# Packed rotary columns, norm sums on VectorE, attention on queries and keys in place, in a two-block transformer kernel

## The chip, the cores and the metric

The kernel runs on one core of a Trainium2 chip. The time is that of the whole program on the device, in microseconds (us). A profiled execution also gives a span, from its first to its last instruction.

## What is computed

Two transformer blocks work on one sequence of 512 tokens of width 1024, all in f32. The first block puts 16 meta tokens in front (528 columns in all). It has an RMS norm, an input projection, an S5 state-space mixer, differential attention with 4 heads, output products, and a gated feed-forward with its own norm. The second block has two layers; each has a norm, an input projection of 28 column blocks, four branches (a conformer convolution, an HGRN2 branch, an SSD branch, latent attention with rotary positions), an output product and a norm of its result. What the change touches:

```python
def rmsnorm(x, g):
    r = lax.rsqrt(jnp.mean(xf * xf, axis=-1, keepdims=True) + EPS)
    return (xf * r).astype(x.dtype) * g
...
    # first block, attention: q and k after their norm, per head two halves of 64
    s = jnp.einsum('bqhjd,bkhjd->bhjqk', q_blk, k)
    p = jax.nn.softmax(s, axis=-1)
    w = p[:, :, 0] - lam * p[:, :, 1]
    o = jnp.einsum('bhqk,bkhe->bqhe', w, v)
...
def apply_rotary(x, positions):      # x: 32 columns; x1, x2 its halves
    out = jnp.concatenate([x1 * cos - x2 * sin, x2 * cos + x1 * sin], axis=-1)
...
def mla_branch(cq, ckv, k_rope, gate, positions, qa_g, qb_w, kva_g, kvb_w):
    q = (rms_norm(cq, qa_g) @ qb_w).reshape(bsz, s, D_HEADS, D_NOPE + D_ROPE)
    q = jnp.concatenate([q[..., :D_NOPE], apply_rotary(q[..., D_NOPE:], positions)], axis=-1)
    k_r = apply_rotary(k_rope, positions)
...
    x = x + rms_norm(y, post_norm_g[l])    # y: the output product of the layer
```

## The kernel before

Activations lie transposed: 128 channels on the partitions, tokens along the free dimension, eight tiles for 1024 channels. The residual is X, the squares and then the normed input are in HN, projections in PJ (PJ2 is the same memory in the second block, 28 tiles of 512 columns), scratch in SC, V and R. Weights stream through `ring`, four slots of 512 KB, which SyncE fills as TensorE frees them. Each engine runs its own hand-written program; the order of its lines is the order of the work, and semaphores tie the engines together. A wait therefore holds everything behind it on its engine. PSUM has eight banks: `put`/`take` wait until one is free, `full`/`got` wait until it is filled.

**A norm's sum** (`norm_sum`, L370) is a product with a matrix of ones, which adds the squares over the partitions: ScalarE squares a tile (`sq_ready`), TensorE adds it into PSUM. In the first block a tile's 528 columns are two halves of 264, and all eight tiles of half 0 come before those of half 1. Then ScalarE takes logarithm and exponential (`root`, L1105 and L1107), and VectorE scales eight tiles (`norm`, L1695), each of which lets TensorE go on. The first call stands at the program's start; VectorE computes angles up to L1742 meanwhile. The second stands behind the first block's output product (L622), whose results VectorE adds to X (L1913) and ScalarE squares (L1314); VectorE then prepares the first feed-forward weights (`sums(0)`, L1923 to L1926).

**Attention of the first block.** ScalarE copies a head's queries and keys out of PJ into QS and KS (`queries`, L1228 and L1229, semaphore `qst`). Per head and per tile of queries (t = 0 has 16, t = 1 to 4 have 128): `score` on TensorE (L505 to L514), VectorE adds the position bias and takes the maximum (L1850, L1854), ScalarE exponentiates (L1247), VectorE combines the two halves (L1868), `turn` transposes the weights (L524), ScalarE copies them (L1254, L1255), `weigh` multiplies by the values (L533). Between these stand `gate_half` products (L490) of the gate projection. Tiles 0 and 1 of the next head are scored inside the loop of this one, so the loop of head 3 scores a fifth head that nobody uses.

**Second block, start of a layer.** `part(j)` (L719) is projection j, 16 instructions, into bank 0 or 1. Projections 0 to 3 are the latent query, the latent key and a mixed tile (time steps in rows 0 to 3, rotary key in rows 64 to 95). `d_sums` sums their squares (L733, L736); ScalarE makes the root; VectorE scales them (L2019, L2020) and posts `d_mul`. The rotary needs the key with its halves swapped: a product with the matrix `rot` (L958), which ScalarE copies to R (L1433, `d_kr`). `d_query(h)` makes a head's query (L742, 96 rows) and, in a second pair of products, its swapped rotary part (L747, 32 rows), each in its bank; ScalarE copies both (L1381, L1383). GpSimd multiplies by cosine and sine and adds (L1636 to L1643): first the key, then each head's query. Behind this come projections 6 to 9, keys and values. VectorE meanwhile starts on the convolution's 31 taps (L2253, L2033, L2035) as soon as ScalarE has evacuated projection 7, and gives attention its first scores (L2042) after 14 of them.

**Second block, end of a layer.** The output product has eight tiles (L1065). ScalarE squares each from PSUM into PJ2 (L1574, `y_sq`) and copies it to HN (L1575). Behind each tile but the first, TensorE adds the squares of the tile before with a `ones` product (L1071); the last one is L1073. ScalarE then takes the root (L1577, L1579), and VectorE and GpSimd update X.

Of the kernel before, what the change touches and what calls it, by code (L numbers as in the profile page):

```python
# [49 lines left out]
CONSTS = [("ident", P), ("ones", P), ("pair64", P), ("mult", 28), ("lvl", 256), ("rot", P), ("dist", T), ("mlamask", SEQ), ("causal", P),  # L50
# [44 lines left out]
def build(nc, a, out):  # L95

    with ExitStack() as ctx:
# [24 lines left out]
        for name in ("par_in", "cst_in", "sc_far", "g_full", "ones_in", "eps_ready", "v_zero", "v_ready", "s5_dt", "ys_gelu",  # L122
# [3 lines left out]
                     "o_root", "o_norm", "glu_th", "ys_ready", "mix_ready", "h_ready", "ffa", "ffc", "ffg", "hid_done", "small_in",  # L126
                     "b_tok", "a_sq", "gate_th", "c_th", "c_x", "c_acb", "c_cme", "d_root", "d_qe", "d_trig_arg", "d_trig", "d_q",
                     "d_sc", "d_ex", "d_wt", "yo", "y_sq", "pos_in", "qst", "a_act", "a_dve", "a_mul", "b_act", "b_dve", "b_mul",
                     "b_zero", "c_act", "c_dve", "c_in", "c_mul", "c_tok", "d_kr", "d_misc", "d_mul", "d_tok", "d_tr", "g_used",
                     "par2_in", "w2_free", "x1_ready", "x2_e", "x2_o", "y_done", "sa_ready", "tb_ready", "snap", "ff_p", "ff_u", "g_free0", "g_free1"):  # L130
# [62 lines left out]
        QS = cut(T)  # L193
        KS = cut(T)
# [96 lines left out]
        def bank(b):  # L291

            return PS[b // 2][:, b % 2, :]
# [49 lines left out]
        def _(pe):  # L343
# [19 lines left out]
            def norm_sum(t0=0, halves=2, width=H):  # L363

                put(0, False)
                for h in range(halves):
                    for k in range(KD):
                        if h == 0:
                            pe.wait_ge(*n("sq_ready"))
                        ins = mm(PS[0][:, h, 0:width], c("ones"), HN[:, k, t0 + h * width:t0 + (h + 1) * width],  # L370
                                 start=(k == 0), stop=(k == KD - 1))
                ins.then_inc(SEMS["act_full0"], 1)
                n("hn_ready", KD)
# [123 lines left out]
            def score(t):  # L497
# [42 lines left out]
            pe.wait_ge(*n("qst"))  # L540
            score(0)
            score(1)
# [4 lines left out]
            for h in range(HEADS):  # L547
                g = 3 + 3 * h
                score(2)
                gate_half(g, 0)  # L550
                turn(0)
                score(3)
# [3 lines left out]
                score(4)  # L556
# [7 lines left out]
                pe.wait_ge(*n("qst"))  # L564
                score(0)
# [3 lines left out]
                score(1)  # L569
# [58 lines left out]
            norm_sum()  # L628
# [73 lines left out]
            for l in range(LAYERS):  # L702
# [35 lines left out]
                def d_query(h):  # L738
                    x, y = (6, 7) if h % 2 == 0 else (2, 3)
# [1757 lines left out]
```

## Time and profile before

| | us |
|---|---|
| median of 3 runs | 1708.13 (1707.27 to 1710.15) |
| profiled execution, its own time | 1707.5 |
| its span | 1705.7 |
| TensorE (PE) busy | 1629.5, 96% |
| VectorE (DVE) busy | 745.9, 44% |
| ScalarE (ACT) busy | 421.9, 25% |
| GpSimd (POOL) busy | 116.7, 7% |

The 1.8 us between the profiled execution's time and its span lie outside the first and last instruction. A matmul on f32 shows as two MATMUL rows, one for each of two instructions, and a row's duration runs from start to modelled end; consecutive ones overlap, so their busy time is not the sum of durations. The rows "PEld" are weight loads, which overlap the matmuls.

### The profile page before, as it was taken

The numbers are of one execution on the slowest core, as the hardware profiler recorded it, in microseconds if no ns is written. First come the engines' busy times: TensorE is split into PE (matmuls) and PEld (weight loads), VectorE is DVE, ScalarE is ACT, GpSimd is POOL, SyncE is SP. The second block draws the span as 40 slices with busy tenths as digits, with TensorE's granted clock in tenths as the row PEclk, the third lists the DMA queues.
The fourth block names the chain that finished last, engine by engine and source line by source line (L and its number), as shares of the span: only waits on it lengthen the run. The fifth ranks groups of instructions, "written<-read, shape, count | busy, mean of one in ns | idle before, by whom it ended". The sixth has DMA issues, their size and how long they took to land.

```text
span 1705.7 us, 16217 instructions
## 1 busy us (share of the span) xinstructions
PE 1629.5 (96%) x6364; PEld 1031.9 (60%) x6364; DVE 745.9 (44%) x1267; ACT 421.9 (25%) x823; POOL 116.7 (7%) x82
## 2 busy tenths in 40 slices
PE   7999999999989999999999998999998998999996
PEld 6884677778878888884443434555543434555542
DVE  8537433322137676762002047765303147765302
ACT  3652544430011010101001131242412131242321
POOL 4014000000000000000000050001001050001001
PEclk9999999999999999999999999999999999999998
DMA  5211111322212222222222212112121211111121
GB/s 203 65 38 48 49 49 50 101 90 74 73 39 81 93 83 90 85 89 86 75 74 61 63 37 62 38 50 63 49 63 38 74 37 56 44 50 38 37 74 49
DMA packets 31660, 111.60 MB, mean 65 GB/s; under 512 B 3520, under 2 KB 3776, under 8 KB 31072
## 3 DMA queue, kind: packets, MB, share of 16 engines
q1 hardware_dynamic: 31248, 108.32, 20.4%
q0 software_dynamic: 336, 2.23, 0.4%
q8 instruction: 51, 0.84, 0.2%
q14 instruction: 25, 0.20, 0.0%
HBM read 108.45 MB, written 2.10 MB: 65 GB/s over the span
## 4 chain that ended last, share of the span: by engine, by line
PE 90%; DVE 6%; ACT 2%; issue 1%; ACTq 1%; DMA 0%; POOL 0%; DVEq 0%; SPq 0%
PE PS L719 21%; PE PS L645 16%; PE PS L675 9%; PE PS L1065 6%; PE PS L490 6%; PE PS L390 5%; PE PS L609 3%; PE PS L622 3%; PE PS L466 2%; DVE SC L2035 2%; PE PS L811 2%; PE PS L370 1%; PE PS L768 1%; PE PS L747 1%; PE PS L784 1%; PE PS L742 1%
## 5 line engine op out<-in xcount | busy, mean ns | idle before, releaser
L719 PE MATMUL PS<-HN,ring 128*128 128x512 f32 x896 | 407.8, 605 | 4.9 <-DVE HN L1695 4.9
L719 PEld LDWEIGHTS PS<-HN,ring 128*128 128x128 f32 x896 | 168.9, 193 | 204.6 <-issue 199.7
L675 PE MATMUL PS<-PJ,ring 128*128 128x512 f32 x352 | 151.3, 592 | 1.9 <-DVEq L1679 1.9
L645 PE MATMUL PS<-SC 128*128 128x257 f32 x528 | 123.6, 383 | 2.0 <-issue 2.0
L675 PEld LDWEIGHTS PS<-PJ,ring 128*128 128x128 f32 x352 | 66.8, 190 | 86.0 <-issue 83.7
L1065 PE MATMUL PS<-PJ,ring 128*128 128x512 f32 x256 | 112.1, 592 | 0.0
L645 PEld LDWEIGHTS PS<-SC 128*128 128x128 f32 x528 | 101.3, 192 | 17.3 <-issue 2.4
L490 PE MATMUL PS<-HN,ring 128*128 128x264 f32 x448 | 107.0, 393 | 2.2 <-ACT PJ L1209 2.2
L390 PE MATMUL PS<-HN,ring 128*128 128x264 f32 x448 | 103.3, 391 | 2.5 <-DVE HN L1695 2.5
L390 PEld LDWEIGHTS PS<-HN,ring 128*128 128x128 f32 x448 | 85.6, 192 | 18.6 <-issue 2.9
L490 PEld LDWEIGHTS PS<-HN,ring 128*128 128x128 f32 x448 | 84.1, 192 | 19.7 <-issue 3.7
L2035 DVE SCALAR_TENSOR_TENSOR SC<-SC 128x512 f32<-128x512 f32 x120 | 84.8, 749 | 2.6
L1065 PEld LDWEIGHTS PS<-PJ,ring 128*128 128x128 f32 x256 | 48.6, 190 | 61.2 <-issue 61.2
L645 PE MATMUL PS<-HN,ring 128*128 128x257 f32 x352 | 81.6, 382 | 2.4 <-DVE HN L1695 2.4
L1326 ACT ACTIVATE SC<-PS 128x257 f32<-128x257 f32 x44 | 17.0, 386 | 240.2 <-PE PS L645 240.2
L645 PEld LDWEIGHTS PS<-HN,ring 128*128 128x128 f32 x352 | 66.1, 190 | 14.4 <-issue 2.7
L1993 DVE TENSOR_TENSOR X<-X,PS 128x1024 f32<-128x1024 f32 x4 | 4.9, 1221 | 139.4 <-PE PS L675 139.4
L622 PE MATMUL PS<-PJ,ring 128*128 128x264 f32 x256 | 57.2, 386 | 1.7 <-DVEq L1679 1.7
L609 PE MATMUL PS<-PJ,ring 128*128 128x264 f32 x256 | 57.2, 386 | 1.5 <-DVE PJ L1892 1.5
L2350 DVE SCALAR_TENSOR_TENSOR PJ<-HN,V,R 128x512 f32<-128x512 f32 x8 | 5.9, 743 | 119.4 <-ACT R L1579 119.4
L622 PEld LDWEIGHTS PS<-PJ,ring 128*128 128x128 f32 x256 | 48.6, 190 | 10.4 <-DVEq L1679 2.1
L609 PEld LDWEIGHTS PS<-PJ,ring 128*128 128x128 f32 x256 | 48.6, 190 | 10.2 <-DVE PJ L1892 1.9
(420 smaller groups left out, 2091.6 us busy)
## 6 DMA issues: line engine op xcount, KB each, us to landing
ring<-wst SPq DMA_DIRECT2D x188, 512.0 KB, 3.6
X<-xT SPq DMA_DIRECT2D x16, 264.0 KB, 5.4
V<-small POOLq DMA_DIRECT2D x2, 1024.0 KB, 5.2
outT<-X SPq DMA_DIRECT2D x8, 256.0 KB, 2.1
consts<-cst SPq DMA_DIRECT2D x1, 1291.5 KB, 13.5
V<-s5w SPq DMA_DIRECT2D x1, 1280.0 KB, 10.3
POS<-pos SPq DMA_DIRECT2D x1, 256.0 KB, 13.7
params<-par SPq DMA_DIRECT2D x1, 209.5 KB, 2.6
```

The source lines that it names most:

```text
L370: ins = mm(PS[0][:, h, 0:width], c("ones"), HN[:, k, t0 + h * width:t0 + (h + 1) * width], start=(k == 0), stop=(k == KD - 1))
L390: ins = mm(PS[p][:, h, 0:H], ring[:, k % 4, b * P:b * P + P], HN[:, b, h * H:h * H + H], start=(b == 0), stop=(b == KD - 1))
L466: ins = mm(PS[t // 2][0:rows, t % 2, :], HN[:, b, q0:q0 + rows], ring[:, b // 2, (b % 2) * 512:(b % 2) * 512 + 512], start=(b == 0), stop= ...
L490: ins = mm(PS[h][:, 1, 0:H], ring[:, k % 4, b * P:b * P + P], HN[:, b, h * H:h * H + H], start=(b == 0), stop=(b == KD - 1))
L609: ins = mm(PS[p][:, h, 0:H], ring[:, s, (4 * x + b) * P:(4 * x + b) * P + P], src, start=(b == 0), stop=(b == 3))
L622: ins = mm(PS[k][:, h, 0:H], ring[:, s, b * P:b * P + P], PJ[:, 12 + b, h * H:h * H + H], start=(b == 0), stop=(b == KD - 1))
L645: ins = mm(PS[bnk // 2][:, bnk % 2, 0:257], left[:, b * P:b * P + P], right[:, b, :], start=(b == 0), stop=(b == 3))
L675: ins = mm(PS[m // 2][:, m % 2, :], ring[:, s, m * P:m * P + P], hid[:, k, :], start=start, stop=stop)
L719: ins = mm(bank(b), ring[:, r, i * P:i * P + P], HN[:, i, 0:SEQ], start=(i == 0), stop=(i == KD - 1))
L811: ins = mm(o, BK[rows, cc, t * P:t * P + P], q, start=True, stop=True)
L1065: ins = mm(bank(j % 2), ring[:, j % WSLOTS, b * P:b * P + P], PJ2[:, src, :], start=(x == 0), stop=(x == KD - 1))
L2035: ins = stt(CA[:, cc, :], x, w1, CA[:, cc, :], ALU.mult, ALU.add)
```

## The change

It has four parts.

1. **Norm sums.** The first `norm_sum` runs tile by tile with both halves of a tile together. For the feed-forward's norm and for the norm of the output product, VectorE adds the squares of tiles 0 to 6 into tile 6 (six additions each), and TensorE multiplies only tiles 6 and 7 by ones. New semaphores `sq_sum` and `y_sum` say when tile 6 holds the sum. The `ones` products between output products go.
2. **Attention of the first block** reads queries and keys from PJ. `queries`, QS, KS and `qst` go, and head 3 no longer scores a fifth head.
3. **Rotary key.** The mixed weight tile has the swapped key columns in columns 96 to 127, so projection 3 gives both. `rot` and its product go; ScalarE copies the rows in the evacuation of projection 3, and `d_kr` goes with its wait on GpSimd.
4. **Rotary queries.** The swapped parts of the four heads are packed into 128 columns and made by one pair of products (`d_swapped`, bank 5) ahead of the queries; ScalarE copies them in four pieces of 32 rows (`swapped`). Each `d_query(h)` keeps one pair, and the heads use banks 6, 7, 2, 3.

```diff
-            def norm_sum(t0=0, halves=2, width=H):
+            def norm_sum(added=0):
                 put(0, False)
...
+                for k in range(added, KD):
+                    if k == added and added:
+                        pe.wait_ge(*n("sq_sum"))
+                        n("sq_ready", KD - 1)
+                    else:
+                        pe.wait_ge(*n("sq_ready"))
+                    for h in range(2):
+                        ins = mm(PS[0][:, h, 0:H], c("ones"), HN[:, k, h * H:(h + 1) * H], start=(k == added), stop=(k == KD - 1))
...
-                q = [QS[64 * j:64 * j + 64, q0:q0 + rows] for j in range(2)]
-                kk = [KS[64 * j:64 * j + 64, :] for j in range(2)]
+                q = [PJ[64 * j:64 * j + 64, 4 + head, q0:q0 + rows] for j in range(2)]
+                kk = [PJ[64 * j:64 * j + 64, 8 + head, :] for j in range(2)]
...
-                pe.wait_ge(*n("qst"))
-                score(0)
+                if h + 1 < HEADS:
+                    score(h + 1, 0)
...
-            norm_sum()
+            norm_sum(KD - 2)
...
                 def d_query(h):
-                    x, y = (6, 7) if h % 2 == 0 else (2, 3)
+                    x = (6, 7, 2, 3)[h]
...
+                def d_swapped():
+                    take(5)
                     for b in range(2):
+                        ins = mm(bank(5), SW[:, SWR + b * P:SWR + b * P + P], CQ[:, b, :], start=(b == 0), stop=(b == 1))
+                    ins.then_inc(SEMS["ba5"], 1)
...
-                take(4)
-                mm(bank(4), c("rot"), PJ2[:, 16, :], start=True, stop=True).then_inc(SEMS["ba4"], 1)
                 pe.wait_ge(*n("small_in", 16))
                 pe.wait_ge(*n("d_mul"))
+                d_swapped()
...
-                    if i:
-                        pe.wait_ge(*n("y_sq"))
-                        mm(bank(2), c("ones"), PJ2[:, i - 1, :], start=(i == 1), stop=False)
-                pe.wait_ge(*n("y_sq"))
+                pe.wait_ge(*n("y_sum"))
+                mm(bank(2), c("ones"), PJ2[:, KD - 2, :], start=True, stop=False)
+                pe.wait_ge(*n("y_sq", KD))
                 mm(bank(2), c("ones"), PJ2[:, KD - 1, :], start=False, stop=True).then_inc(SEMS["ba2"], 1)
...
-            def queries(h):
-                af(QS[:, :], PJ[:, h + 4, :], ACT.Copy)
-                af(KS[:, :], PJ[:, h + 8, :], ACT.Copy).then_inc(SEMS["qst"], 1)
...
+                def swapped():
+                    full(5)
+                    for h in range(HEADS):
+                        ins = af(QR[rr, h, :], bank(5)[32 * h:32 * h + 32], ACT.Copy, scale=-(QKR ** -0.5))
+                    released(ins, 5)
...
-                evac(3, 16)
+                full(1)
+                af(PJ2[:, 16, :], bank(1), ACT.Copy)
+                released(af(KRR[rr, :], bank(1)[96:128], ACT.Copy), 1)
...
-                pool.wait_ge(*n("d_kr"))
...
+                    done = i * 4 + k
+                    if done == 0:
+                        n("sq_ready", KD)
+                    if done:
+                        dve.wait_ge(*n("sq_ready"))
+                    if done > 1:
+                        link(tt(HN[:, done - 1, :], HN[:, done - 1, :], HN[:, done - 2, :], ALU.add))
+            post("sq_sum")
...
+                dve.wait_ge(*n("y_sq"))
+                for k in range(1, KD - 1):
+                    dve.wait_ge(*n("y_sq"))
+                    link(tt(PJ2[:, k, :], PJ2[:, k, :], PJ2[:, k - 1, :], ALU.add))
+                post("y_sum")
+                n("y_sq")
                 dve.wait_ge(*n("rms_root"))
...
+        misc[:, 96:128] = misc[:, 64:96][:, swap]
```

The instruction streams show two places. TensorE, layer 0 of the second block, between projection 5 and projection 7 (L742 queries, L747 their swapped parts before, L749 the packed ones now, L958 `rot`):

```order
 L719 MATMUL PS<-HN,ring 128x512 x16
-L958 MATMUL PS<-PJ,consts 128x512
-L742 MATMUL PS<-PJ,V 96x512 x2
-L747 MATMUL PS<-PJ,V 32x512 x2
-L742 MATMUL PS<-PJ,V 96x512 x2
-L747 MATMUL PS<-PJ,V 32x512 x2
+L749 MATMUL PS<-PJ,V 128x512 x2
+L742 MATMUL PS<-PJ,V 96x512 x4
 L719 MATMUL PS<-HN,ring 128x512 x8
```

Nine products between the projections became six; behind the second projection eight became four. TensorE in head 3 of the first block's attention (L505, L511 scores, L533 values, L524 transposes, L490 gates):

```order
 L490 MATMUL PS<-HN,ring 128x264 x8
-L505 MATMUL PS<-SC 16x16
-L511 MATMUL PS<-SC 16x16
 L533 MATMUL PS<-V,SC 128x128 x4
 L524 MATMUL PS<-consts,SC 128x128 x5
 L490 MATMUL PS<-HN,ring 128x264 x8
-L505 MATMUL PS<-SC 128x144
-L511 MATMUL PS<-SC 128x144
 L533 MATMUL PS<-V,SC 128x128 x5
 L490 MATMUL PS<-HN,ring 128x264 x16
```

The scores that nobody uses are gone, and with them VectorE's and ScalarE's work on them, which stood ahead of the combination that the transposes of tile 4 (L524 x5) wait for.

## Rows read from the trace of the kernel before

**Rows 1.** The page, parts 1 and 4: the engines, and the chain that ended last.
```profile
PE 1629.5 (96%) x6364; PEld 1031.9 (60%) x6364; DVE 745.9 (44%) x1267; ACT 421.9 (25%) x823; POOL 116.7 (7%) x82
...
PE 90%; DVE 6%; ACT 2%; issue 1%; ACTq 1%; DMA 0%; POOL 0%; DVEq 0%; SPq 0%
```

**Rows 2.** TensorE's waits: line <- what ended them: us in total, times, longest.
```profile
PE PS L768 <- DVE SC L2042: 4.6, 2, 2.3
```

**Rows 3.** The chain of waits, output products of layer 0: start us, us, what.
```profile
1254.23 6.87 PE PS L1065 x16
1261.95 6.87 PE PS L1065 x16
```

**Rows 4.** The norm of the feed-forward: the chain, then the timeline.
```profile
487.23 7.13 PE PS L370 x32
...
488.06 0.64 ACT L1314 ACTIVATE HN<-X 128x528 f32<-128x528 f32 x1 [6.48 <-DVEq L1675]
488.18 0.69 DVE L1923 TENSOR_TENSOR SC<-ring 128x512 f32<-128x512 f32 x1 [0.20 <-issue]
```

**Rows 5.** Timeline of layer 0's output products, ScalarE: start us, us, engine, line.
```profile
1292.03 0.60 ACT L1574 ACTIVATE PJ<-PS 128x512 f32<-128x512 f32 x1 [6.64 <-PE PS L1065]
```

**Rows 6.** The chain of waits, layer 0: the `rot` product, heads 0 and 1.
```profile
979.97 0.86 PE PS L958 x2
980.83 1.72 PE PS L742 x4
982.55 1.83 PE PS L747 x4
...
988.10 7.07 PE PS L719 x16
```

**Rows 7.** Timelines of layer 0 by engine: ScalarE, VectorE (DVE), GpSimd (POOL).
```profile
981.99 0.59 ACT L1433 ACTIVATE R<-PS 32x512 f32<-32x512 f32 x1
...
969.50 0.74 DVE L2020 SCALAR_TENSOR_TENSOR PJ<-PJ,V,SC 128x512 f32<-128x512 f32 x1
...
1010.21 1.23 DVE L2253 SCALAR_TENSOR_TENSOR SC<-PJ 128x1024 f32<-128x1024 f32 x1 [23.68 <-ACTq L1087]
...
985.53 5.30 POOL L1638 TENSOR_TENSOR PJ<-PJ,R 32x2048 f32<-32x2048 f32 x1
...
1005.80 1.26 POOL L1643 TENSOR_TENSOR SC<-SC,PJ 32x512 f32<-32x512 f32 x1
```

**Rows 8.** Timeline of head 0: the value products of tile 2 and their wait.
```profile
230.20 0.74 PEld L533 LDWEIGHTS PS<-V,SC 128*128 128x128 f32 x6 [0.46 <-ACT SC L1255]
```

**Rows 9.** The chain of waits, head 3 of the first block's attention.
```profile
333.48 0.12 PE PS L505
...
335.58 0.77 PE PS L524 x5
336.35 3.56 PE PS L490 x16
339.91 0.32 PE PS L505
```

**Rows 10.** Timeline of the first norm and what follows it.
```profile
6.52 9.94 PE L370 MATMUL PS<-HN,consts 128*128 128x264 f32 x32 [6.52 <-ACT HN L1114]
...
8.76 3.37 ACT L1114 ACTIVATE HN<-X 128x528 f32<-128x528 f32 x5 [0.68 <-DMA X<-xT]
...
15.19 0.39 DVE L1742 TENSOR_SCALAR SIN<-SIN 128x448 f32<-128x448 f32 x1
16.49 0.70 ACT L1105 ACTIVATE R<-PS,epsc 128x528 f32<-128x528 f32 x1 [4.36 <-PE PS L370]
...
18.02 4.17 DVE L1695 SCALAR_TENSOR_TENSOR HN<-X,params,R 128x528 f32<-128x528 f32 x6 [2.45 <-ACT R L1107]
```

**Rows 11.** All cores; busy time and granted clock (PEclk) of a stretch.
```profile
core 0: 1705.7 us, clock 0.984
...
17.00:24.00 7.00, 5.07 (x13) 3.35 (x14) 5.98 (x9) 6.66 (x9) 1.31 (x2) 0.77 0.75 302
```

More of the change, by code:

```diff
@@ L49 @@
         ("bng", 2), ("ccw", 24), ("ccb", 6), ("dtb", 1), ("alog", 1), ("dsk", 2), ("cng", 2), ("qag", 2), ("kvg", 1), ("isl", 1)]
-CONSTS = [("ident", P), ("ones", P), ("pair64", P), ("mult", 28), ("lvl", 256), ("rot", P), ("dist", T), ("mlamask", SEQ), ("causal", P),
+CONSTS = [("ident", P), ("ones", P), ("pair64", P), ("mult", 28), ("lvl", 256), ("dist", T), ("mlamask", SEQ), ("causal", P),
           ("negslope", HEADS + 1), ("invf", 1), ("sgn", 1), ("sel4", 4 * P), ("keep", SEQ)]
@@ L539, in _ @@
             pe.wait_ge(*n("qk_n"))
-            pe.wait_ge(*n("qst"))
-            score(0)
-            score(1)
+            score(0, 0)
+            score(0, 1)
             put(0, False)
@@ L548, in _ @@
                 g = 3 + 3 * h
-                score(2)
+                score(h, 2)
                 gate_half(g, 0)
                 turn(0)
-                score(3)
+                score(h, 3)
                 gate_half(g, 1)
@@ L555, in _ @@
                 turn(1)
-                score(4)
+                score(h, 4)
                 gate_half(g + 1, 0)
@@ L568, in _ @@
                 gate_half(g + 2, 1)
-                score(1)
+                if h + 1 < HEADS:
+                    score(h + 1, 1)
                 weigh(h, 4)
@@ L744, in d_query @@
                     ins.then_inc(SEMS[f"ba{x}"], 1)
-                    take(y)
+                def d_swapped():
+                    take(5)
                     for b in range(2):
-                        ins = mm(bank(y)[64:96], SW[:, SWR + (2 * h + b) * 32:SWR + (2 * h + b + 1) * 32], CQ[:, b, :],
-                                 start=(b == 0), stop=(b == 1))
-                    ins.then_inc(SEMS[f"ba{y}"], 1)
+                        ins = mm(bank(5), SW[:, SWR + b * P:SWR + b * P + P], CQ[:, b, :], start=(b == 0), stop=(b == 1))
+                    ins.then_inc(SEMS["ba5"], 1)
                 def d_keys(g):
@@ L1283, in _ @@
                 exps(4)
-                queries(h + 1)
                 turned(2)
@@ L1289, in _ @@
                 gate(g + 2, 0)
-                exps(0)
+                if h + 1 < HEADS:
+                    exps(0)
                 weighed(h, 3)
@@ L1293, in _ @@
                 gate(g + 2, 1)
-                exps(1)
+                if h + 1 < HEADS:
+                    exps(1)
                 weighed(h, 4)
@@ L1431, in _ @@
                 af(R[0:4, 0:SEQ], R[0:4, 0:SEQ], ACT.Ln, bias=epsc[0:4, 2:3]).then_inc(SEMS["c_act"], 1)
-                full(4)
-                released(af(KRR[rr, :], bank(4)[rr], ACT.Copy), 4)
-                mark("d_kr")
+                swapped()
                 query(0)
@@ L1881, in _ @@
                 combine(3)
-                scores(h + 1, 0)
+                if h + 1 < HEADS:
+                    scores(h + 1, 0)
                 combine(4)
-                scores(h + 1, 1)
-            dve.wait_ge(*n("ex_ready", 2))
+                if h + 1 < HEADS:
+                    scores(h + 1, 1)
             dve.wait_ge(*n("o_root"))
@@ L2433, in layout @@
     r = np.arange(P)[:, None]
-    rot = np.zeros((P, P), np.float32)
-    for k in range(16):
-        rot[64 + 16 + k, 64 + k] = 1.0
-        rot[64 + k, 64 + 16 + k] = 1.0
     dist = r - (np.arange(T)[None] - (SEQ - P + NMETA))
```

31 lines of the change are left out of this document (9 added, 22 removed).

## The prediction, made before the run

> **What bounds it now.** I read the page first: TensorE is busy for 96% of the span and carries 90% of the chain that ended last, VectorE 6% [rows 1]. So a TensorE product that goes away shortens the run unless a wait takes its place, and the list of TensorE's waits says where that could be: 4.6 us stand before the first scores of the second block (L768), for VectorE [rows 2]. Then I read the chain stretch by stretch for what one product costs, and the timelines at five places for who is late there.
>
> **The price of one product.** The page's mean of a 128x512 matmul (592 to 605 ns) is its latency, and consecutive ones overlap. What counts is the step from start to start. An output product of eight f32 products is 16 instructions and 6.87 us, and with one `ones` product behind it the next one starts 7.72 us later [rows 3]. So a product of 512 columns is two instructions and 0.86 us. One of 264 columns costs 7.13/16 = 0.45 us [rows 4]. The Trainium skill, page "TensorE: Matmul & The Clock Gate", section "Back-to-back issue gap", gives N/2.4 + 2.5 ns for one isolated matmul: 216 ns at 512 columns, 0.43 us for two instructions. By that figure the first two terms below would be 12.0 us in place of 23.9; the trace disagrees with it by a factor of two for these f32 operands, and I go by the trace.
>
> **Term 1, output norm: 10.3 us.** In each layer 8 `ones` products become 2; the six removed ones stood in line between output products: 2 x 6 x 0.86. VectorE gets six 128x512 additions per layer, 0.69 us each by its nearest row (L1923) [rows 4]. What hides them is the output product: ScalarE squares tile 6 at 1292.03 for 0.60 us [rows 5], so the sixth addition ends near 1293.4. TensorE needs it after the last output product, near 1299, which will be some 5 us sooner, as tile 6 is too: 5 us of slack either way. The tail behind the last output product (L1071, L1073, square of tile 7 beside the first of them) is the same in both. If the cover were gone, one addition of 0.7 us per layer would be paid.
>
> **Term 2, queries: 13.6 us.** Before, the `rot` product and the first two heads take 979.97 to 988.10, 8.13 us [rows 6]: one product, then four pairs of 1.72 to 1.89 us, together 7.27. Now the same stretch has six products (swapped, head 0, head 1): 5.16 us, 2.97 less. Heads 2 and 3 lose two of their four pairs: 7.27 to 3.44, 3.83 less. Per layer 6.8, in two layers 13.6. What could wait instead:
> - The wait for `d_mul` moves up by the `rot` product. Its last VectorE product starts at 969.50 and takes 0.74 [rows 7]; needed at 979.97, slack 9.7 us. ScalarE's extra copy before `d_misc` delays the chain to it by one 0.59 us copy. GpSimd no longer waits for `d_kr` and starts near 965 in place of 982.8; its wide addition of 5.30 us [rows 7] then lies beside those three VectorE products. Even if they waited for all of it, they would end near 975. Hidden.
> - ScalarE: before, the rotated-key copy starts at 981.99 [rows 7]. Now four quarter copies stand there (2.4 us at 0.59 each), then two query copies: done near 985.7, before the next projection ends near 992. Hidden; no bank is asked for sooner than that, since heads 2 and 3 use banks 2 and 3.
> - The taps: VectorE starts them with L2253 at 1010.21, right behind ScalarE's copy of projection 7, and works through them until the scores [rows 7]. TensorE waits 2.3 us per layer for that (L768) [rows 2]. The start follows TensorE, so it moves by 6.8 us and the wait stays as it is.
> - GpSimd's last rotary row ends at 1007.06, 3.2 us ahead of the taps [rows 7]. Now: head 0 can start near 985.1, heads 0 and 1 take 3.75 us each, head 2 is copied at 994.8, so the last ends near 1002.4, and the taps start near 1003.4. Margin 1 us; see the third rival.
>
> **Term 3, attention of the first block: 3.5 us.** The ten `queries` copies leave ScalarE. They matter once per head: the value products wait 0.46 us for ScalarE (L1255) [rows 8], whose copy of the weights stands behind the two `queries` copies. Four heads: 1.8 us, of which the last belongs to the part below too; I count 4 x 0.46. In head 3 the unused scores of a fifth head go: the chain runs from their first matmul at 333.48 through VectorE's scores and combination to the transposes at 335.58 and the gate at 336.35 [rows 9], 2.87 us. Without it VectorE combines tile 4 some 4 us earlier, under the gate products, and what is left is the five transposes, 0.77 us by their row, and the four value products before them, 0.9 us at that rate: 1.2 less. The second score goes with its 0.45 us (0.32 [rows 9] and the 0.12 behind it). Sum 1.8 + 1.2 + 0.5 = 3.5. Reading queries and keys from PJ in place of a copy has no row. Bounds: from nothing to a gain of nothing, since the same matmuls read and write the same shapes; taken as 0. At the start of attention the copies stand in front of ScalarE's S5 copy, but that one waits for TensorE: nothing.
>
> **Term 4, first norm: 2.4 us.** The loops are swapped, so only two products stand behind the last square instead of nine. The squares end at 12.13 (8.76 + 3.37) [rows 10]. TensorE's sixteen products (7.1 us) now run beside them from 6.52 and end near 13.9 instead of 16.4. Logarithm and exponential then end near 15.3, but VectorE is only free at 15.58, so the scaling starts at 15.6 instead of 18.02 [rows 10]. 2.4 us, not 3.1: VectorE is late next.
>
> **Term 5, norm of the feed-forward: 3.5 us.** Before, sixteen products (7.13 us) run from 487.23. Now TensorE waits for VectorE's last addition: the last square starts at 488.06, the addition of 0.7 us starts beside it, and four products of 0.45 follow from 488.9 to 490.7. Root 3.6 us earlier; with hand-offs 3.5. The earlier five additions lie under output products of 7.1 us. `sums(0)` now starts 0.7 us later and ends near 491.7, before the root.
>
> **Sum.** 10.3 + 13.6 + 3.5 + 2.4 + 3.5 = 33.3. The profiled execution took 1707.5 us, of which the span is 1705.7; less 33.3 is 1674.2. The median of the runs shown is 0.6 higher, so I predict **1674.8 us**, a gain of 1.9%. Unknown costs at their ends: term 1 8.9 to 10.3, term 2 11.5 to 14, term 3 1.4 (only the ScalarE waits) to 4.5, term 4 0 (if a DMA sets the pace behind it) to 3.1, term 5 1.8 to 3.6. Together 23.6 to 35.5, so 1672.6 to 1684.5.
>
> **The clock.** After the 2.4 us idle before the first projections the granted clock drops: 0.77 in the mean of 17 to 24 us [rows 11], which is 1.6 us lost to the lower level, 1.2 GHz. Over the run 0.984 is granted [rows 11], 27 us less than full, some 16 such drops, part of them in idle time. Shifted work meets them elsewhere. The wait of term 5 is a new idle stretch followed at once by another and may add one. I allow three drops either way, 5 us: my range is **1668 to 1682**.
>
> **Rivals.**
> 1. *The clock eats it, slower than before.* Every place where TensorE waits could be followed by a drop of 1.6 us. Twenty-one more drops cancel the gain; 23 make it slower by over 0.2%, 1674.8 + 23 x 1.6 = 1712. Against it: the change removes more idle time (terms 3 and 4) than it adds (term 5), and of the waits that stay most are followed by no drop now. The same page of the Trainium skill, section "HAM oscillation", tells of a kernel that lost to such drops at every wait; no run here shows it yet. 1%.
> 2. *A removed product is worth half* (0.43 us, the rate by the skill's figure above): 1674.8 + 12 = 1687. Against it the 7.72 us step. 2%.
> 3. *GpSimd spills into the taps.* If the rotary rows do not move up at all, they end 3.7 us behind the start of the taps, and in the worst case hold VectorE for that time in each layer: 1674.8 + 7.4 = 1682. It decides from the point where the last rotary row ends behind L2253. The Trainium skill, page "SBUF — State Buffer", section "SBUF: two separate sides", says that a VectorE operation with two SBUF inputs and one of GpSimd lock each other out for a whole instruction; by that rule the full 3.7 us would be lost. My sum leaves 1 us of room. 6%.
> 4. *A new wait behind term 4 or 5* (a DMA, ScalarE's block copies) swallows both: 1681. 6%.
> 5. *The change does not do what it says*: no mechanism leaves TensorE its removed products, since they are gone from its stream. Below 1%, 1708.
>
> **Chances.** The forecast holds with 84%, rivals 3 and 4 with 12%, 2 with 2%; rival 1 and 5 with 1% each. A measurement of this kernel tells 0.2%, 3.4 us, from no change. Faster by more 0.98, within 0.01, slower 0.01.
>
> **What would show it.** In the profile after: output products that follow each other in 6.87 us; swapped, heads 0 and 1 in 5.2 us; no wait for L1255's successor in attention and none before the last transposes of head 3; the first projections starting at 16.5; the root of the second norm 3.5 us after the last output product instead of 7.1; taps starting 6.8 us sooner per layer with the 2.3 us wait unchanged. The prediction is wrong if TensorE's waits grow by more than 5 us, or if the mean clock falls below 0.98.

## The result, and the profile after

| | before | changed |
|---|---|---|
| median, us | 1707.7 (4 runs, 1705.87 to 1710.15) | 1683.2 (4 runs, 1674.88 to 1683.49) |
| ratio | | 0.9848, 95% interval 0.9833 to 0.9864 |
| span of the profiled execution, us | 1705.7 | 1681.4 |
| granted clock there | 0.984 | 0.980 |

The kernel is 24.5 us faster where 33.3 were forecast. The median lies 8.4 us above the predicted 1674.8 and 1.2 us above the end of the range; one run of the four, 1674.88, met the forecast. The page's engines and chain, to set beside [rows 1]:

```profile
PE 1603.7 (95%) x6280; PEld 1023.5 (61%) x6280; DVE 763.3 (45%) x1279; ACT 414.7 (25%) x805; POOL 117.1 (7%) x82
...
PE 89%; DVE 6%; ACT 2%; issue 1%; ACTq 1%; DMA 0%; POOL 0%; DVEq 0%; SPq 0%
```

TensorE has 84 instructions less and is still the bound. Its waits (line <- what ended them: us in total, times, longest):

```profile
PE PS L949 <- ACT SC L1562: 7.2, 2, 3.6
PE PS L371 <- ACT HN L1113: 7.1, 1, 7.1
PE PS L706 <- ACT HN L1351: 5.9, 2, 4.8
PE PS L785 <- DVE SC L2057: 5.3, 4, 2.4
PE PS L719 <- DVE HN L1693: 4.9, 2, 2.5
PE PS L769 <- DVE SC L2049: 4.7, 2, 2.3
PE PS L524 <- DVE SC L1866: 2.6, 3, 0.9
PE PS L371 <- DVEq L1677: 1.9, 1, 1.9
```

The wait before the second block's first scores (L769) is 4.7 us, against 4.6 in [rows 2]. The value products (L533) no longer wait for ScalarE, where they waited four times and 1.8 us before. One wait is new, L371 for VectorE's last sum (1.9 us), and was forecast. The longest ones, at the start aside, are as long as before. So no wait took the gain. The chain of waits (start us, us, what) at the places of [rows 3, 4, 6, 10]:

```profile
7.07 9.77 PE PS L371 x32
19.29 30.31 PE PS L390 x128
...
486.51 2.03 PE PS L371 x8
490.89 5.36 PE PS L645 x16
...
972.43 1.72 PE PS L749 x4
974.15 3.43 PE PS L742 x8
977.59 6.87 PE PS L719 x16
984.45 3.43 PE PS L742 x8
...
1229.51 54.93 PE PS L1065 x128
```

The eight output products are now one piece, 54.93/8 = 6.87 us each, and swapped, head 0 and head 1 take 1.72 + 3.43 = 5.15 us: terms 1 and 2 stand as worked out. Two things don't. The first projection (L390) starts at 19.29, where 16.5 was forecast and 18.93 stood before. And some stretches that did not change got longer. Each layer has a wait of 3.60 us before the gated norm's sums (L948, now L949). In the first layer it ends like this, before and then after (timeline, TensorE):

```profile
1230.78 1.99 PE L948 MATMUL PS<-SC,consts 128*128 128x512 f32 x4 [3.60 <-ACT SC L1563]
1232.61 7.03 PE L719 MATMUL PS<-HN,ring 128*128 128x512 f32 x16
```
```profile
1217.73 3.78 PE L949 MATMUL PS<-SC,consts 128*128 128x512 f32 x4 [3.60 <-ACT SC L1562]
1221.31 8.20 PE L719 MATMUL PS<-HN,ring 128*128 128x512 f32 x16
```

The four products take 3.78 us instead of 1.99, and the sixteen instructions behind them 8.20 instead of 7.03. The granted clock of a stretch behind the wait (PEclk is the third number from the right), before and after:

```profile
1231.00:1234.40 3.40, 3.40 (x9) 1.48 (x9) 0.00 (x0) 2.17 (x3) 0.00 (x0) 1.00 0.00 0
```
```profile
1218.00:1221.40 3.40, 3.40 (x5) 1.32 (x6) 0.00 (x0) 0.69 (x1) 0.00 (x0) 0.50 0.00 0
```

It is 1.00 before and 0.50 after, the upper and the lower of the two levels: a drop of the clock at a wait that had none in this layer. The lower level holds from 1216.8, still in the wait, to 1223.6. From the end of the wait to the end of the sixteen instructions 11.78 us pass instead of 8.86. The next rows show a shorter drop, behind a wait of 2.37 us that both kernels have (L784 before, L785 after):

```profile
1057.04 3.65 PE L719 MATMUL PS<-HN,ring 128*128 128x512 f32 x8
```
```profile
1042.30 5.35 PE L719 MATMUL PS<-HN,ring 128*128 128x512 f32 x8
```

This drop costs 1.7 us, the one at L949 2.9. For every run I use two numbers below. **Withheld** is span x (1 - granted clock). **At full clock** is span x granted clock, what is left. The clock has three decimals, so both are good to 0.8 us for one run, and a mean is hardly better where the runs read the same decimals: differences below a microsecond tell nothing. A low clock in an idle stretch counts as withheld and costs nothing; the last 12.5 us before and 14.0 us after are such a stretch, TensorE idle at the lower level, so 6 to 7 us of these figures for withheld cost nothing, and 5.5 to 7 in the profiles of the other kernels. Before: 26.7 withheld and 1678.4 at full clock (mean of 17 runs). Changed: 31.9 and 1647.5 (mean of the four: 33.6, 33.6, 25.1 and 35.3 withheld). So 30.9 us were gained at full clock; of these 5.2 went back to the clock in the mean, and 33.6 - 26.7 = 6.9 in the run at the median.

The two profiles can be counted drop by drop. Ahead of that last stretch, the kernel before is at the lower level ten times, 41.0 us together; the changed kernel eleven times, 54.6 us. Two drops are gone, those at 20.7 and 505.4. Three are new: at 1042.7 (L785), at 1216.8 (L949) and at 1305.6. Two have become twice as long, at 199.7 and 1394.3. While TensorE was at work, 18.6 us were withheld before and 24.0 after, so the clock took 5.4 us of real work. The spans differ by 24.3, which leaves 33.3 - 24.3 - 5.4 = 3.6 us for everything else.

### The profile page after: what moved, and what is told of

The parts are those of the page before. It is cut to its first block, busy times and chain, and to the rows that moved or that the text cites. A ratio compares the mean times of both kernels' runs of the same rounds, so it can differ in the third digit from the quotient of the medians.

```text
span 1681.4 us, 16052 instructions
## 1 busy us (share of the span) xinstructions
PE 1603.7 (95%) x6280; PEld 1023.5 (61%) x6280; DVE 763.3 (45%) x1279; ACT 414.7 (25%) x805; POOL 117.1 (7%) x82
## 4 chain that ended last, share of the span: by engine, by line
PE 89%; DVE 6%; ACT 2%; issue 1%; ACTq 1%; DMA 0%; POOL 0%; DVEq 0%; SPq 0%
PE PS L719 21%; PE PS L645 16%; PE PS L675 9%; PE PS L1065 7%; PE PS L490 6%; PE PS L390 5%; PE PS L622 3%; PE PS L609 3%; PE PS L466 2%; DVE SC L2042 2%; PE PS L812 2%; PE PS L769 1%; PE PS L592 1%; PE PS L785 1%; ACT PJ L1146 1%; PE PS L742 1%
## 5 line engine op out<-in xcount | busy, mean ns | idle before, releaser
L719 PE MATMUL PS<-HN,ring 128*128 128x512 f32 x896 | 412.9, 611 | 4.9 <-DVE HN L1693 4.9
L719 PEld LDWEIGHTS PS<-HN,ring 128*128 128x128 f32 x896 | 171.5, 196 | 207.5 <-issue 202.4
L645 PEld LDWEIGHTS PS<-SC 128*128 128x128 f32 x528 | 100.1, 190 | 16.8 <-issue 2.4
L490 PE MATMUL PS<-HN,ring 128*128 128x264 f32 x448 | 107.9, 396 | 2.2 <-ACT PJ L1208 2.2
L390 PE MATMUL PS<-HN,ring 128*128 128x264 f32 x448 | 102.7, 388 | 2.5 <-DVE HN L1693 2.5
L490 PEld LDWEIGHTS PS<-HN,ring 128*128 128x128 f32 x448 | 84.9, 194 | 19.9 <-issue 3.7
L390 PEld LDWEIGHTS PS<-HN,ring 128*128 128x128 f32 x448 | 84.2, 190 | 19.3 <-issue 2.9
L645 PEld LDWEIGHTS PS<-HN,ring 128*128 128x128 f32 x352 | 66.1, 190 | 14.4 <-issue 2.7
## 6 DMA issues: line engine op xcount, KB each, us to landing
consts<-cst SPq DMA_DIRECT2D x1, 1227.5 KB, 13.6
```

The lines of the kernel that those rows point to most:

```text
L390: ins = mm(PS[p][:, h, 0:H], ring[:, k % 4, b * P:b * P + P], HN[:, b, h * H:h * H + H], start=(b == 0), stop=(b == KD - 1))
L490: ins = mm(PS[h][:, 1, 0:H], ring[:, k % 4, b * P:b * P + P], HN[:, b, h * H:h * H + H], start=(b == 0), stop=(b == KD - 1))
L645: ins = mm(PS[bnk // 2][:, bnk % 2, 0:257], left[:, b * P:b * P + P], right[:, b, :], start=(b == 0), stop=(b == 3))
L719: ins = mm(bank(b), ring[:, r, i * P:i * P + P], HN[:, i, 0:SEQ], start=(i == 0), stop=(i == KD - 1))
```

## The experiments

My theory: terms 1, 2, 3 and 5 hold, term 4 fails because TensorE is slow in its first microseconds, and the rest of the gap is drops of the clock behind waits that stayed. The rivals: a part is worth less than I said; or one pays for it elsewhere. All medians below are beside runs of the kernel before on the same chip, whose own medians were 1707.1, 1706.95, 1707.38 and 1707.25 in the four groups of runs.

| kernel | median, range, runs | ratio to before, 95% | at full clock | withheld |
|---|---|---|---|---|
| output norm sums alone | 1699.3, 1698.5 to 1701.2, 5 | 0.9959, 0.9946 to 0.9971 | 1668.6 | 29.2 |
| rotary columns alone | 1695.1, 1689.1 to 1696.4, 6 | 0.9922, 0.9907 to 0.9937 | 1664.1 | 27.6 |
| attention in place alone | 1703.8, 1701.1 to 1704.5, 11 | 0.9980, 0.9972 to 0.9989 | 1675.3 | 26.4 |
| feed-forward norm sums alone | 1704.9, 1702.9 to 1706.9, 11 | 0.9990, 0.9982 to 0.9999 | 1675.4 | 27.9 |
| changed, first norm's loops as before | 1680.0, 1674.9 to 1682.5, 4 | 0.9839, 0.9823 to 0.9856 | 1647.8 | 29.8 |
| changed, again | 1682.3, 1681.4 to 1683.7, 4 | 0.9856, 0.9842 to 0.9869 | 1646.6 | 34.0 |
| changed, filled waits, first try | 1681.7, 1681.5 to 1682.1, 4 | 0.9851, 0.9836 to 0.9866 | 1663.2 | 16.8 |
| changed, filled start, two products | 1683.0, 1675.3 to 1683.3, 4 | 0.9848, 0.9830 to 0.9866 | 1647.0 | 32.3 |
| changed, filled waits, fitted | 1667.9, 1663.9 to 1668.5, 4 | 0.9763, 0.9750 to 0.9777 | 1654.0 | 11.2 |
| the same and filled start, four | 1663.7, 1662.2 to 1664.5, 5 | 0.9745, 0.9731 to 0.9758 | 1652.1 | 9.6 |
| the same, first norm's loops as before | 1668.8, 1663.6 to 1669.0, 5 | 0.9762, 0.9750 to 0.9775 | 1654.7 | 10.7 |
| before, filled waits and start | 1698.6, 1693.4 to 1701.8, 6 | 0.9949, 0.9937 to 0.9960 | 1684.8 | 11.9 |

The last two columns are means over the runs.

### One part at a time

**The output norm's sums alone**, on the kernel before:

```diff
-                    if i:
-                        pe.wait_ge(*n("y_sq"))
-                        mm(bank(2), c("ones"), PJ2[:, i - 1, :], start=(i == 1), stop=False)
-                pe.wait_ge(*n("y_sq"))
+                pe.wait_ge(*n("y_sum"))
+                mm(bank(2), c("ones"), PJ2[:, KD - 2, :], start=True, stop=False)
+                pe.wait_ge(*n("y_sq", KD))
...
+                for k in range(1, KD - 1):
+                    dve.wait_ge(*n("y_sq"))
+                    link(tt(PJ2[:, k, :], PJ2[:, k, :], PJ2[:, k - 1, :], ALU.add))
```

> The kernel before (1707.7 us) with the output norm's sums alone. Theory: twelve products of 512 columns leave TensorE at 0.86 us each, VectorE's twelve additions are hidden: 10.3 us less, 1697.4; output products follow each other in 6.87 us; at full clock 1678.4 becomes 1668.1. Rival 1 (a product is worth half): 5.2 us less, 1702.5. Rival 2 (the clock takes it back where the work is shifted): time 1700 to 1706 while the figure at full clock still falls by 10.

At full clock 1678.4 - 1668.6 = 9.8 us less, against 10.3. The clock withheld 2.5 more, so the median fell by 7.8 only. That is 0.82 us per product, its whole step of 0.86 within the error, and not half of it.

**The rotary columns alone** (`d_swapped`, four heads on banks 6, 7, 2, 3, no `rot`, no `d_kr`):

```diff
-                take(4)
-                mm(bank(4), c("rot"), PJ2[:, 16, :], start=True, stop=True).then_inc(SEMS["ba4"], 1)
                 pe.wait_ge(*n("small_in", 16))
                 pe.wait_ge(*n("d_mul"))
+                d_swapped()
```

> The kernel before with the packed rotary columns alone (key and queries). Theory: 6.8 us per layer, 13.6 less, 1694.1; at full clock 1678.4 becomes 1664.8; the taps' first VectorE row stands 6.8 us earlier and TensorE's wait before the first scores of each layer stays 2.3 us. Rival (GpSimd spills into the taps): that wait grows by up to 3.7 us per layer and the time is 1694 to 1701.

14.3 us less at full clock, 13.6 expected, and the wait before the first scores is 4.6 us for both layers, as before. The rival is out. In the changed kernel GpSimd's last rotary row ends at 993.26 + 1.26 = 994.52 and the taps start 0.93 us later (timeline, POOL and DVE):

```profile
993.26 1.26 POOL L1641 TENSOR_TENSOR SC<-SC,PJ 32x512 f32<-32x512 f32 x1
...
995.45 1.23 DVE L2260 SCALAR_TENSOR_TENSOR SC<-PJ 128x1024 f32<-128x1024 f32 x1 [18.39 <-ACTq L1086]
```

**Attention in place alone**, without a fifth head's scores:

```diff
-                q = [QS[64 * j:64 * j + 64, q0:q0 + rows] for j in range(2)]
-                kk = [KS[64 * j:64 * j + 64, :] for j in range(2)]
+                q = [PJ[64 * j:64 * j + 64, 4 + head, q0:q0 + rows] for j in range(2)]
+                kk = [PJ[64 * j:64 * j + 64, 8 + head, :] for j in range(2)]
```

> The kernel before with attention reading queries and keys in place and without the scores of a fifth head, nothing else. Theory: 3.5 us less, 1704.2, at full clock 1674.9; TensorE's waits on ScalarE's weight copy (L1255) fall from 0.46 us each to near nothing. Rival (reading in place costs something, or the clock takes it): no change at full clock, or a loss of granted clock of more than 3 us.

3.1 us less at full clock, 3.5 expected, and TensorE's waits for ScalarE's weight copy are gone: reading in place costs nothing that can be told.

**The feed-forward norm's sums alone:** `norm_sum(KD - 2)` there and VectorE's six sums beside the last output products.

> The kernel before (1707 us) with the sums of the feed-forward norm alone. Theory: sixteen products become four, the new wait for VectorE is 1.9 us, so 3.2 us less: 1704, at full clock 1675.2 against 1678.4. Rival (the new idle stretch brings a drop of the clock of its own, or the next wait takes it): same time, and either a clock below 1 in 480 to 500 us or a longer wait of L645 than 2.4 us.

2.9 us less at full clock (1678.3 to 1675.4), 3.2 expected. The median fell by 2.1, since 1.3 more was withheld. The new wait brought no drop of its own: in this profile, as in the changed kernel's, the clock is 1.00 from 480 to 510 us, where the kernel before had its drop at 505.4. Other kernels with this wait do show one near it, at 491.1 with the first norm's loops taken back (below).

**The first norm's loops, taken back** in the changed kernel:

```diff
-                for k in range(added, KD):
...
+                for h in range(2):
+                    for k in range(KD):
+                        if h == 0:
+                            pe.wait_ge(*n("sq_ready"))
```

> The changed kernel (1683.2 us, 1674.9 in one of its four runs) with the first norm's sixteen products in the order of before. Theory: TensorE steps through its first products at 0.445 us each where later ones of the same size take 0.22, so the products, not the loop order, set the end of the first norm and the reordering bought nothing: 1683 us, within 1.5 us of the changed kernel, the first projection (L390) starts between 18.8 and 19.4 us. Rival (the prediction's term 4 holds and something else took its place): 2.4 us slower than the changed kernel, 1685.6, first projection later than 21 us. In both, TensorE's clock may move the whole by 8 us either way, so I compare at full clock: span times granted clock is 1647.8 by the theory, 1650.2 by the rival.

1647.8 against 1646.6 and 1647.5 at full clock. The first projection stands at 18.57 in this profile, 0.2 outside the expected 18.8 to 19.4, because the first input landed sooner: the norm starts at 6.60, not 7.07. From the norm's start it is 11.97 us with the old loops and 12.22 with the new. The changed kernel's second profile has 12.06, and the first projection at 18.71. The new loop order bought about nothing.

**The changed kernel again**, for its kinds of run:

> The changed kernel again, beside the three others, for a better count of its two kinds of run. By the theory every run has span times clock between 1647 and 1649, whatever its time; about three of four near 1683 and one near 1675. By the rival (the first four runs were chance) one group around 1680.

All four near 1682, with 33.6 to 35.3 withheld and 1646.1 to 1647.0 at full clock. Of eight runs in the two comparisons seven took 1681.4 to 1683.7 and one 1674.88, with 25.1 withheld and 1648.0 at full clock. What differs between executions of this kernel is the clock, and within 2 us nothing else. The expected 1647 to 1649 was 1 us too high for these four.

### Is it the clock? Filling the waits

The products below read constants and write a bank that nobody reads before it is overwritten. They change no result; where they fit into a wait they cost nothing but keep TensorE at work.

```diff
+            def warm(o, n_):
+                for _ in range(n_):
+                    mm(o, c("ones"), cst[:, 0:264] if o.shape[-1] == 264 else c("keep"), start=True, stop=True)
...
             score(0, 0)
+            warm(PS[3][:, 1, 0:H], 2)
             score(0, 1)
+            warm(PS[3][:, 1, 0:H], 4)
             put(0, False)
```

> The changed kernel with products of constants that nobody reads, placed into nine of TensorE's waits (before the first projections of each norm, at the start and end of the first attention, before the first scores and one of the value products of the second block, before the recurrence's output). Theory (the missing microseconds are drops of the clock behind waits, 33.6 us at the lower level in three of four runs): the clock rises to 0.99 or more, span times clock stays 1648 (up to 3 us more where a product overshoots its wait), time 1660 to 1668. Rival (drops come at random, or from what runs elsewhere on the chip): clock 0.980 to 0.986 as before, 1675 to 1686.

The clock rose to 0.990 and the four runs lie within 0.6 us, but the time did not fall: 1681.7. That was not the theory's 1660 to 1668. The time is the rival's, the clock is not. The timeline shows why (the added lines shift the numbers: L785 is L804 here, L949 is L971, and L349 is the products of constants):

```profile
1037.18 1.99 PE L349 MATMUL PS<-consts 128*128 128x512 f32 x4 [2.28 <-DVE SC L2082]
1039.00 1.00 PE L804 MATMUL PS<-SC,PJ 128*128 128x64 f32 x8
```
```profile
1217.81 3.58 PE L971 MATMUL PS<-SC,consts 128*128 128x512 f32 x4 [3.60 <-ACT SC L1587]
```

The bank I had chosen came free only when the wait was over, so two products stood behind it, on the path. And those meant for the longest wait stood in front of the recurrence's output, not of L971, whose 3.60 us stayed open with a drop at its end. The next kernel mends this:

```diff
                 def d_weigh(h, t):
                     if h == 0 and t == 3:
-                        s, uses = n.now("bf5")
+                        s, uses = n.now("bf6")
                         pe.wait_ge(s, uses)
-                        warm(bank(5), 2)
+                        warm(bank(6), 2)
...
                 def c_out():
-                    s, uses = n.now("bf6")
-                    pe.wait_ge(s, uses)
-                    warm(bank(6), 3)
...
                 def c_sums():
+                    s, uses = n.now("bf4")
+                    pe.wait_ge(s, uses)
+                    warm(bank(4), 4)
```

> The run before filled the waits but made eleven products too many: three per layer in front of the recurrence's output, where TensorE does not wait (L949 is the gated norm's sum product, not the output as I had taken it), two per layer on a bank that came free only with the wait (L785), one before the second block's first norm; 11 x 0.86 = 9.5 us. Now these are gone or moved to a free bank, and four products stand before L949. Theory: 1681.7 - 9.5 = 1672, and two drops less behind L949 (3.4 us): 1669, range 1666 to 1673, clock 0.99 or more, the runs within 2 us of each other. Rival (full-rate TensorE only waits longer, so the clock was never worth the difference between 1683 and 1675): 1675 or more.

1667.9, within the theory's 1666 to 1673 and 14.4 us below the changed kernel; the rival is out. The four runs are 4.7 us apart, though, where 2 were expected. And the products of constants aren't free: at full clock this kernel stands at 1654.0, 7 us above the changed kernel, so of 22.8 us less withheld (34.0 to 11.2) 14.4 arrived.

### The start

> The changed kernel with two such products before the first norm's. Theory: TensorE's low rate at its start (0.445 us per instruction) ends some 2 us sooner, so the first projection starts about 1 us earlier, 18.3 instead of 19.3 us; the whole 1682, or 1674 in the faster kind of run. Rival (the low rate belongs to these products, not to the engine's first microseconds): first projection at 19.3 or later.

The first projection starts at 19.02, where 18.3 was expected, and the time did not change. The changed kernel alone has 19.29 in one profile and 18.71 in the other, so these two products moved nothing that can be told. Between them and the norm's first product TensorE was idle for 1.56 us. With four products instead of two, and the fitted waits:

```diff
             pe.wait_ge(SEMS["ones_in"], 16)
+            warm(PS[0][:, 0, 0:H], 4)
             norm_sum()
```

> The same, and four products of constants before the first norm's, so that TensorE has no gap between 3.3 us and its first square. With two of them the first projection started 0.3 us earlier, not 1 us; a gap of 1.6 us was left before the first square. Theory (that gap let the low rate start over): the low rate ends near 9 us of the span, the first projection starts at 17.5 to 18.3, and the time is 1 to 1.7 us below the run without them. Rival (the low rate lasts until some 12 us whatever TensorE does): first projection at 19.0 or later, no difference.

The first projection starts at 17.07: 2.2 us sooner than in the first profile of the changed kernel, 0.8 sooner than with the fitted waits alone (17.89). The kernel takes **1663.7 us**, the fastest of this study: 2.5% below before, where the change alone gave 1.5%. It is 4.2 us below the fitted waits alone, where 1 to 1.7 were expected; 1.9 of them stand at full clock. Where L949's wait of 3.60 us stood, TensorE now works, and no drop follows (L972 is L949 here):

```profile
1205.08 3.60 PE L349 MATMUL PS<-consts 128*128 128x512 f32 x8
1208.85 1.99 PE L972 MATMUL PS<-SC,consts 128*128 128x512 f32 x4 [0.17 <-ACT SC L1588]
```

The low rate at the start shows in the number of TensorE instructions in a stretch, though not in the clock column (the third number from the right, 1.00 everywhere). The changed kernel, then this one:

```profile
7.00:12.00 5.00, 4.93 (x12) 3.90 (x13) 4.42 (x20) 4.32 (x7) 0.00 (x0) 1.00 1.03 382
12.00:14.40 2.40, 2.40 (x12) 2.07 (x11) 2.23 (x6) 0.18 (x1) 0.00 (x0) 1.00 1.05 432
```
```profile
7.00:12.00 5.00, 4.75 (x21) 4.10 (x22) 4.42 (x20) 4.42 (x8) 0.00 (x0) 1.00 1.02 389
12.00:14.40 2.40, 2.40 (x12) 2.07 (x11) 2.23 (x6) 0.20 (x1) 0.00 (x0) 1.00 1.06 437
```

Twelve instructions of 264 columns touch the 5.0 us and then twelve the 2.4 us. One of them is cut by the border of the stretch, so the steps are near 5.0/11 = 0.45 and 2.4/11 = 0.22 us. With the four products ahead it is 21 in the same 5.0 us. The 1.00 in the column says nothing here: the trace of the changed kernel has no record of the clock before 11.9 us, which is where the step changes, and this kernel's first record stands at 6.3 us. In the profiles of kernels without the four products ahead the first record stands between 9.9 and 13.0 us, with them at 6.3, 7.3 and 8.6. The Trainium skill, page "TensorE: Matmul & The Clock Gate", section "Part 1: The HAM clock gate", says that the throttled clock is the default and activity releases it; by that rule the first products of a kernel are slow. The steps of 0.45 and then 0.22 us agree.

**Does the loop order pay at full rate?** The fastest kernel with the loops of before:

> The fastest kernel so far (1663.7, products of constants in the waits and ahead of the first norm) with the first norm's sixteen products in the order of before. Theory (the loop order is worth something only once TensorE runs at full rate there, which it does now): the second halves' eight products stand behind the last square, so the first projection starts 1.5 to 2.5 us later than 17.07 and the time is 1665.5. Rival (the loop order is worth nothing at any rate): 1663.7, first projection within 0.5 us of 17.07.

The first projection starts at 18.64, 1.57 us later than 17.07, and 2.6 us are lost at full clock. The median is 5.1 higher, where 1.8 was expected: the five runs take 1663.6 to 1669.0, and the clock has its part. ScalarE's wait from the last square to the root tells the order's worth best: it is 4.36 us with the old order, here as in the kernel before, and 2.45 with the new one in the fastest kernel (4.68 in the changed kernel, where TensorE was late). So term 4 is real, about 2 us, and was only out of reach. The two norms (timeline, old order, then new order):

```profile
8.56 7.70 PE L380 MATMUL PS<-HN,consts 128*128 128x264 f32 x28 [0.35 <-ACT HN L1144]
16.10 1.50 PE L349 MATMUL PS<-consts 128*128 128x264 f32 x6
18.64 5.69 PE L402 MATMUL PS<-HN,ring 128*128 128x264 f32 x17 [1.05 <-DVE HN L1724]
```
```profile
7.25 7.36 PE L375 MATMUL PS<-HN,consts 128*128 128x264 f32 x32 [0.38 <-ACT HN L1139]
14.45 1.50 PE L349 MATMUL PS<-consts 128*128 128x264 f32 x6
17.07 7.25 PE L397 MATMUL PS<-HN,ring 128*128 128x264 f32 x24 [1.12 <-DVE HN L1719]
```

**Is the whole change worth its forecast once the clock is kept up?** The kernel before with the same products in the same places:

> The kernel before with the same products of constants in the same places. Theory (the five parts are worth their sum wherever the clock is kept up, term 4 too; the shortfall against the forecast was the clock's): 32 to 34 us above the changed kernel with these products, 1696 to 1698. Rival (the products of constants cure something that only the kernel before or only the changed one had): before gains as much from them as the changed kernel did, 19 us, to 1688, or the difference stays at the 24.5 us first measured.

1698.6 against 1663.7: 34.8 us between the medians, where 32 to 34 were expected, and 1684.8 - 1652.1 = 32.7 at full clock. The forecast's sum was 33.3. The runs of this kernel are 8.4 us apart, so its median is the less certain of the two. The same products gave before 8.7 us and the changed kernel 18.6 to 19.5. Before had less withheld to win back (27.1 to 11.9, that is 15.2; the changed kernel 34.0 to 9.6, 24.4).

## Why the prediction was right, and where it was not

- **What bounds it**: right. TensorE lost 84 instructions and the time followed; no new bound.
- **The price of one product**: right, 0.86 us. Term 1 measured 9.8 of 10.3; the second rival (half the worth, 1687) is out at full clock, where its term 1 would be 5.2.
- **Term 2**: 14.3 of 13.6. Its hidden work stayed hidden, the wait before the first scores did not move, and the third rival's margin came out at 0.93 us where I had 1.
- **Term 3**: 3.1 of 3.5. **Term 5**: 2.9 of 3.5, with the new wait where it was expected.
- **Term 4**: failed. The step that failed is "TensorE's sixteen products (7.1 us) now run beside them from 6.52 and end near 13.9". I took the 7.1 us from the norm of the feed-forward [rows 4], though the row of this very norm said 9.94 [rows 10], as if the rest were waiting for squares. It was TensorE's rate: the sixteen products take 9.77 us in the new order, and 9.51 in the changed kernel with the old one. So TensorE, not the last square, set the end, and the first projection started at 19.29 where 16.5 was forecast. The order became worth something, about 2 us, only with work ahead of it.
- **The clock**: the mechanism was named and its size nearly so, but its sign was argued wrongly. "The change removes more idle time than it adds" was to limit it to three drops either way, 5 us. It withheld 5.2 us more in the mean of the first four runs and 7.4 in the mean of the next four, against an allowance of 5 us, so the median fell just outside the range; one run of four read 0.979, below the 0.98 named as a sign of being wrong. The range was also narrower than its own terms: their bounds gave 1672.6 to 1684.5 before any clock, and it ended at 1682. Two drops did go, those at 20.7 and 505.4. But waits that had not changed, L785 and L949 of the first layer, were met by drops that they did not have before, two other drops doubled in length, and the new wait (term 5) had none in the changed kernel's two profiles. The allowance was also worked out from 27 us taken as some 16 drops; the profile shows ten, two of them of twice the length, and 6 us in the idle end. The four parts alone withheld 2.5, 0.9, -0.3 and 1.3 us more than before, together 4.4.
- **The chances**: rivals 3, 4 and 5 did not come; rival 1 came in part, a sixth to a quarter of the gain and never near all of it. The Trainium skill's page named beside it, "TensorE: Matmul & The Clock Gate", section "HAM oscillation", was the one to take more seriously: by its rule the clock falls behind waits again and again. The profile after agrees at L949 in both layers (3.78 us for 1.99 in the first); the profile before has the same wait of 3.60 us twice, with a drop in the second layer (at 1614.7) and none in the first.

So the account of the 33.3 us: 30.9 arrived at full clock, and the missing 2.4 are about what term 4 did not bring (the other four parts measured 9.8 + 14.3 + 3.1 + 2.9 = 30.1, against their 30.9, the same within the error). In the median the clock took 6.9 of them; 24.5 is what the medians show. Where the clock was kept up in both kernels, 32.7 arrived.

**What stays open.** Why a given wait is followed by a drop in one kernel, in one layer or in one run, and not in another: the waits L949 and L785 have the same length in both kernels. Moving the work changes which waits are hit; no run here shows what decides it. So it is shown that filling the waits gives the clock back, and not shown why this change lost some of it. Two drops, near 1155 and 1534 us in the changed kernel (1168 and 1553 before), stand where no wait does: L719's eight instructions behind L893 take 5.40 us in both kernels, 3.65 elsewhere. No product was placed for them. The first is still there in the fastest kernel, the second is not.

## What to carry to other kernels

Read the granted clock and the span of every run before arguing about 1%: work removed from the bounding engine came off to within a microsecond or so per part, and most of what looked like a missing part of the gain was the clock, in good part at waits that the change never touched. Where such an engine must wait, products of constants into a bank that is already free can stand in the wait. They pay only if they fit: eleven too many gave back all they had won. And take the price of an operation from a row of the same stretch, not of the same shape: in the first microseconds the same product costs twice as much.

## What the runs showed of the hardware that was not expected

- In the changed kernel TensorE steps through its first products at half rate, 0.45 us per instruction of 264 columns against 0.22, from 7.1 to 11.9 us. The clock column of that stretch reads 1.00 only because the trace has no record of the clock yet. With four products of constants ahead the first record stands at 6.3 us.
- Two executions of one kernel differ by 8.3 us (1683.2 and 1674.9) with 1647.8 and 1648.0 at full clock. (The withheld time goes in steps of 1.7 us from run to run, but so does the rounding of the clock to 0.001, and the two can't be told apart.)
- A wait of 2.4 us can be followed by a drop, as L785 shows in the first layer of the changed kernel, and one of 3.6 us need not be, as L948 shows in the first layer before. Two drops follow no wait at all.
- Drops differ in length and price: 3.4 us at the lower level cost 1.7 at L785, 6.8 us cost 2.9 at L949, part of it lying in the wait.
- With the waits and the start filled 9.6 us are withheld in place of 34.0, some 6 of them in the idle end, and five runs lie within 2.3 us.
